# Modulation rows in four column groups of TensorE, shift and scale moved into the evictions, and recurrent columns first in the second input projection

## What is computed

```python
# block 1
mod = silu(c) @ ada_w + ada_b                       # one row of 6 x 1024
sh1, sc1, g1, sh2, sc2, g2 = split(mod, 6)
h = layer_norm(x) * (1 + sc1) + sh1
proj = h @ w_in + b_in                              # 8728 columns: attention inputs and gates
...                                                 # two attentions, merged
x = layer_norm(ALPHA * x + (1 + g1) * (merged @ w_out)) * ln1_g + ln1_b
h = layer_norm(x) * (1 + sc2) + sh2
x = layer_norm(ALPHA * x + (1 + g2) * moe(h)) * ln2_g + ln2_b   # 32 experts, 2 per token
# block 2
p = rms_norm(x) @ w_in_2                            # 256 q, 768 convolution, 1536 recurrent columns
x = x + concat(memory_attention(q), conv(pc), rwkv(pr)) @ w_out_2
x = x + expert_choice_ffn(rms_norm(x))              # 16 experts
out = rms_norm(x)
```

## Time and profile before

| | us |
|---|---|
| median of 3 runs | 2116.62 (2116.36 to 2118.09) |
| profiled execution | 2113.64 |
| its span, first to last instruction | 2111.8 |
| TensorE busy in it | 1617.2 |
| VectorE busy | 566.2 |
| ScalarE busy | 332.0 |
| granted TensorE clock, mean | 0.892 of full |

### The profile page before, as it was taken

How to read it: one execution, slowest core, us unless ns; L and a number is a source line. 1 busy time by engine, 2 the same in 40 slices (tenths; PEclk the granted TensorE clock), 3 DMA queues, 4 the chain that set the end, 5 groups by cost and what they waited for, 6 DMA issues and landing times.

```text
span 2111.8 us, 20549 instructions
## 1 busy us (share of the span) xinstructions
PE 1617.2 (77%) x8115; PEld 902.6 (43%) x8115; DVE 566.2 (27%) x1063; ACT 332.0 (16%) x699; POOL 159.7 (8%) x275
## 2 busy tenths in 40 slices
PE   7999988989978777777774976787786766666664
PEld 2746856776354222222221855566644212122111
DVE  1011243311321221211214047788742000000002
ACT  0101224510012111111111131122202000000000
POOL 3000030000000000000000002213300000000000
PEclk9999988989998999999997986888896888888887
DMA  9742342226361999999997430000002899999995
GB/s 356 182 169 82 111 171 100 71 94 218 107 255 39 428 428 429 428 429 428 429 428 288 144 120 1 1 11 1 1 33 97 353 429 429 427 429 429 428 428 245
DMA packets 84964, 510.90 MB, mean 242 GB/s; under 512 B 9543, under 2 KB 12392, under 8 KB 60326
## 3 DMA queue, kind: packets, MB, share of 16 engines
q1 hardware_dynamic: 80950, 500.21, 58.2%
q0 software_dynamic: 3952, 9.83, 2.0%
HBM read 506.87 MB, written 3.15 MB: 242 GB/s over the span
## 4 chain that ended last, share of the span: by engine, by line
PE 51%; DMA 32%; DVE 7%; issue 5%; ACT 3%; POOL 1%; SPq 1%; DVEq 0%; POOLq 0%; ACTq 0%
PE ps L1130 48%; DMA ring<-in_exp_w 16%; DMA ring<-in_w_e_up 15%; ACT arena L1054 1%; PE ps L1525 1%; POOL arena L706 1%; DMA ring<-in_ada_w 1%; DMA arena<-in_causal 0%; POOL arena L710 0%; DVE stats L1892 0%; DVE vv L2403 0%; PE ps L1160 0%; SPq L532 0%; SPq L570 0%; PE ps L1797 0%
## 5 line engine op out<-in xcount | busy, mean ns | idle before, releaser
L1130 PE MATMUL ps<-ring,arena 128*32 128x512 f32 (+4 forms) x3540 | 559.1, 673 | 203.8 <-DMA ring<-in_w_e_up 105.2
L1130 PEld LDWEIGHTS ps<-ring,arena 128*32 128x32 f32 (+2 forms) x3540 | 169.3, 132 | 549.6 <-issue 400.2
L1130 PE MATMUL ps<-arena 128*128 128x128 f32 (+7 forms) x1320 | 238.3, 354 | 52.0 <-POOL arena L706 21.5
L1130 PE MATMUL ps<-hTs,ring 128*128 128x256 f32 x1088 | 242.9, 384 | 5.9 <-PE ps L1130 3.7
L1130 PEld LDWEIGHTS ps<-hTs,ring 128*128 128x128 f32 x1088 | 208.1, 192 | 40.2 <-issue 11.8
L1130 PEld LDWEIGHTS ps<-arena 128*128 128x128 f32 (+3 forms) x1320 | 177.1, 212 | 104.9 <-issue 46.7
L1525 PE MATMUL ps<-arena 128*128 128x512 f32 x256 | 117.5, 601 | 29.0 <-DVE arena L2179 29.0
L1130 PE MATMUL ps<-ring,hTs 128*128 128x512 f32 (+4 forms) x352 | 118.4, 492 | 8.1 <-ACT hTs L1064 5.8
L2179 DVE COPY arena<-ps 128x512 f32<-128x512 f32 x32 | 22.1, 691 | 339.9 <-PE ps L1130 339.9
L2491 DVE TENSOR_TENSOR arena<-arena,ps 64x512 f32<-64x512 f32 x16 | 11.0, 690 | 357.7 <-ACT arena L1085 357.7
L1130 PEld LDWEIGHTS ps<-ring,hTs 128*128 128x128 f32 x352 | 64.3, 212 | 60.6 <-issue 52.8
(11 more groups left out here) (388 smaller groups left out, 1258.4 us busy)
## 6 DMA issues: line engine op xcount, KB each, us to landing
ring<-in_exp_w SPq DMA_DIRECT2D x96, 2048.0 KB, 20.7
ring<-in_w_e_gate SPq DMA_DIRECT2D x32, 2048.0 KB, 18.8
ring<-in_w_e_up SPq DMA_DIRECT2D x32, 2048.0 KB, 23.3
ring<-in_w_e_down SPq DMA_DIRECT2D x32, 2048.0 KB, 23.8
ring<-in_w_in SPq DMA_DIRECT2D x22, 2048.0 KB, 14.8
ring<-in_ada_w SPq DMA_DIRECT2D x12, 2048.0 KB, 8.5
ring<-in_w_out SPq DMA_DIRECT2D x4, 2048.0 KB, 7.9
ring<-in_w_br_hg SPq DMA_DIRECT2D x2, 2048.0 KB, 14.8
```

What stands on the lines that cost most here:

```text
L1130: return nc.tensor.matmul(o, lhsT, rhs, start=start, stop=stop)
```

## The change

**First part.** The modulation products use four column groups: silu(c) is spread over 32 columns, the eight products of a tile go to four groups of 32 partitions, two each, and the bias row goes to the first group. A bank then holds four partial rows. `mod_columns` turns shift and scale into columns: 16 products of a 128-column piece of the row with one column of ones on partitions 0, 32, 64 and 96, which sums the four and transposes. `mod_rows` does the sum for the gates: two products of 512 columns to all 128 partitions. The whole-matrix modulation on DVE is gone; the transposes take the normalized matrix, and scale and shift are applied per partition when the banks are emptied, two of four banks by ACT and two by DVE. In the compact form of expert stage 1 the gathered tokens get scale and shift at their eviction, too, which moves ACT's 16 evictions into the branch.

The order changes with it: the first transposes stand between the second and third tile, and all eight later tiles stand together ahead of the output projection, with `w_out` behind them in the ring.

**Second part.** In w_in_2 the three tiles with recurrent columns come first, then queries with the first convolution tile, and the last tile (two banks, `in2b`) is computed after `vt`. On DVE `prepare(0, ..)`, the reciprocal and the key's scaling stand ahead of the memory scores. On ACT the first `decays(0)` stands ahead of the memory exponentials. Two buffers move, since `hT` stays in use longer.

```diff
@@ the order of jobs and of weights @@
-PLAN1 = [("mod", 4), ("cols", 1), ("rel", 1), ("hT", 4), ...
+PLAN1 = [("mod", 2), ("hT", 4), ("modb", 2), ("modc", 1), ("cols", 1), ("rel", 1), ...
-         ("g1", 2), ("y", 4), ("mod2", 6), ("memT", 4), ("km", 1), ("vm", 2),
+         ("ada2", 8), ("g1b", 2), ("modc2", 1), ("g2b", 2), ("y", 4), ("memT", 4), ("km", 1), ("vm", 2),
-PLAN2 = [("h3T", 4), ("in2", 10), ...
-         ("kks", 2), ("vt", 2), ("matt", 10), ...
+IN2 = (2, 3, 4, 0, 1)
+PLAN2 = [("h3T", 4), ("in2", 8), ...
+         ("kks", 2), ("vt", 2), ("in2b", 2), ("matt", 10), ...
@@ TensorE @@
-                mm(bank(j), ones_row, brow_at(n)[1], True, False)
+                mm(bank(j, rows=32), ident[0:1, 0:1].to_broadcast([1, 32]), brow_at(n)[1], True, False)
                 for k in range(KC):
-                    ins = mm(bank(j), c[:, k, :], slot(n, (8, 512))[:, k, :], False, k == KC - 1)
+                    q = k % 4
+                    ins = mm(bank(j)[32 * q:32 * q + 32, :], c[:, k, :], slot(n, (8, 512))[:, k, :],
+                             0 < k < 4, k >= 4)
...
+            group = C("fold")[:, 0:1]
+            def mod_columns(name, shift, scale, every):
+                j = job(name)
+                for k in range(KC):
+                    for i, row in enumerate((shift, scale)):
+                        part = row[:, k::KC] if every else row[:, k * P:(k + 1) * P]
+                        ins = mm(bank(j)[:, 8 * i + k:8 * i + k + 1], part, group)
+                fills(ins, j)
+            def mod_rows(name, row):
+                for i in range(2):
+                    j = job(name, i)
+                    fills(mm(bank(j), group.to_broadcast([P, P]), row[:, i * 512:i * 512 + 512]), j)
...
-            for i in range(2):
-                modulation("g1", i, cbc2)
+            for i in range(8):
+                modulation("ada2", i, cbc2)
+            all_out(pe, "ada2", 8)
+            mod_rows("g1b", mod2[:, 0, :])
+            mod_columns("modc2", mod2[:, 1, :], mod2[:, 2, :], True)
+            mod_rows("g2b", mod2[:, 3, :])
             pe.wait_ge(S("merged_ready"), 1)
...
-            for i in range(6):
-                modulation("mod2", i, cbc2)
@@ ScalarE @@
+            act.wait_ge(S("modc_ready"), 1)
+            for j in (0, 2):
+                is_full(act, J("hT", j))
+                for i in range(2):
+                    k = 2 * j + i
+                    ins = nc.scalar.activation(hT[:, k, :], v3(bank(J("hT", j)), 2)[:, i, :], ACT.Identity,
+                                               bias=modc[:, k:k + 1], scale=modc[:, 8 + k:9 + k])
+                frees(ins, J("hT", j))
@@ VectorE @@
-            for t in range(TT):
-                link(stt(xn[:, t, :], mod1[:, 1, :], 1.0, xn[:, t, :], ALU.add, ALU.mult))
-            say(tt(xn[:], xn[:], mid(mod1[:, 0, :], TT), ALU.add), "h_ready")
+            layer_norm(xn, x, "xn_ready")
+            mod_column_pairs(J("modc"), modc)
+            modulated("hT", modc)
...
+            mod_column_pairs(J("modc2"), modc2)
             dve.wait_ge(S("mem_loaded"), 16)
...
+            all_out(dve, "w0", 2)
+            prepare(0, 0)
+            dve.wait_ge(S("kk_roots"), 2)
+            link(nc.vector.reciprocal(KKs, KKs))
+            link(tt(KKn, KKn, KKs, ALU.mult))
+            all_out(dve, "a0", 2)
+            for part in range(1, 4):
+                prepare(0, part)
             mem_scores(0)
             mem_scores(1)
+            all_out(dve, "in2b", 2)
```

More of the change, by code:

```diff
@@ L761, in _ @@
             nc.scalar.activation(lb, lb, ACT.Sigmoid).then_inc(S("lb_sigmoid"), 1)
-            for j in range(4):
-                is_full(act, J("hT", j))
-                frees(nc.scalar.copy(hT[:, 2 * j:2 * j + 2, :], v3(bank(J("hT", j)), 2)), J("hT", j))
             def pair(job, j, dst, func, stack_col):
@@ L880, in _ @@
             for i in range(8):
-                j = J("g1", i) if i < 2 else J("mod2", i - 2)
-                is_full(act, j)
-                frees(nc.scalar.copy(mod2[:, i // 2, (i % 2) * 512:(i % 2) * 512 + 512], bank(j)), j)
+                parts(J("ada2", i), mod2, i)
+            for i in range(2):
+                parts(J("g1b", i), mod2, i)
+            for i in range(2):
+                parts(J("g2b", i), mod2, 6 + i)
             for j in range(4):
@@ L894, in _ @@
                 frees(nc.scalar.copy(vm[:, t, :], bank(J("vm", t), 256)), J("vm", t))
-            for j in range(4):
+            act.wait_ge(S("modc_ready"), 2)
+            for j in (0, 2):
                 is_full(act, J("h2T", j))
-                frees(nc.scalar.copy(hT[:, 2 * j:2 * j + 2, :], v3(bank(J("h2T", j)), 2)), J("h2T", j))
+                for i in range(2):
+                    k = 2 * j + i
+                    ins = nc.scalar.activation(hT[:, k, :], v3(bank(J("h2T", j)), 2)[:, i, :], ACT.Identity,
+                                               bias=modc2[:, k:k + 1], scale=modc2[:, 8 + k:9 + k])
+                frees(ins, J("h2T", j))
             act.wait_ge(S("route_max"), 1)
@@ L903, in _ @@
             frees(nc.scalar.copy(combT, bank(J("combT"), T, NE1)), J("combT"))
-            for i in range(16):
-                is_full(act, J("comb", i))
-                frees(nc.scalar.copy(WB[:, 2 * i:2 * i + 2, :], v3(bank(J("comb", i)), 2)), J("comb", i))
             def silus(turn, at):
@@ L919, in _ @@
             with act.If(fits > 0):
+                for i in range(16):
+                    k = i // 2
+                    is_full(act, J("comb", i))
+                    frees(nc.scalar.activation(XE1[:, k, (i % 2) * 512:(i % 2) * 512 + 512], bank(J("comb", i)),
+                                               ACT.Identity, bias=modc2[:, k:k + 1], scale=modc2[:, 8 + k:9 + k]),
+                          J("comb", i))
                 with act.Fori(0, NE1 // 2) as i:
@@ L928, in _ @@
             with act.If(fits < 1):
+                for i in range(16):
+                    is_full(act, J("comb", i))
+                    frees(nc.scalar.copy(WB[:, 2 * i:2 * i + 2, :], v3(bank(J("comb", i)), 2)), J("comb", i))
                 silus(0, 0)
@@ L960, in _ @@
             nc.scalar.activation(PF[:, 11, :], PF[:, 11, :], ACT.Sigmoid).then_inc(S("tanh_ready"), 1)
+            is_full(act, J("in2", 6))
+            frees(nc.scalar.copy(qa, v3(bank(J("in2", 6)), 2)), J("in2", 6))
+            is_full(act, J("in2", 7))
+            frees(nc.scalar.copy(CA[:, 0:2, :], v3(bank(J("in2", 7)), 2)), J("in2", 7))
             def low_rank(name, dst, func, stack_col):
@@ L2321, in _ @@
             mem_scores(3)
-            prepare(0, 0)
             mem_probs(2)
-            dve.wait_ge(S("kk_roots"), 2)
-            link(nc.vector.reciprocal(KKs, KKs))
             for c in range(3):
```

134 lines of the change are left out of this document (77 added, 57 removed).

## The result

The changed kernel takes 2065.89 us (median of 4 runs, 2064.03 to 2070.15), against 2116.49 for the one before in the same session: a ratio of 0.9763, 95% interval 0.9745 to 0.9781. Forecast were 2063.4 and a range of 2052 to 2081. The ratios leave out two executions that stand far apart from their fellows, one of `part1` at 4980.15 us and one of the kernel before, in the same session, at 2224.27. The profiled execution has a span of 2068.3 us, 43.5 less than the 2111.8 of before.

What follows compares the result with a forecast made beforehand. TensorE's path ahead of the expert stages, which run as fast as weights arrive, was taken as the bound. Gains of 16.2 + 25.3 + 11.7 = 53.2 us off the 2116.62 median gave 2063.4 us, range 2052 to 2081.

Steps and rivals of the forecast that it cites:

- Price of a tile: One modulation tile of ada_w on TensorE: 3.25 us with column groups instead of 8.46; 6.5 at 1.2 GHz.
- Place one: Ahead of the first projection: it starts at 42.8 instead of 60.02; less 1.0 of clock, gain 16.2 us.
- Place two: Between branch products and router: h2 transposes start at 592.5, not 618.80; less 1.0 of clock, gain 25.3 us (16 to 30).
- a lone tile lands in 7.9: At place two: ada 8's weights, issued at 507.6, land 7.9 us later, before TensorE has finished ada 7.
- Columns, 5.6: Each column job turning shift and scale into columns takes 5.6 us at mixed clock; 3.9 at full, 7.2 at low.
- VectorE next in line, covered by 1.8: At place two: normalizing the residual twice takes 16.9 us, under TensorE's 18.7 by 1.8.
- Place three: Between second input projection and scan: low-rank products and scores start earlier, work leaves the memory attention; gain 11.7 us (9 to 13).
- Low clock throughout: Rival: all modulation tiles at 6.5 us; place two loses 1.6, place one gains 10.4; total 2096 us; chance 0.07.
- Weights one at a time: Rival at place two: transfers of ada 8 to 11 don't overlap, each 7.9 us behind the last; 2071 us; chance 0.10.
- Place three moves its wait: Rival: memory scores wait for DVE, its queue having the preparation first; only some 3 us remain; 2072 us; chance 0.10.
- Columns nearly free: Rival: one moving column costs only its issue, both column jobs vanish at most; 2052 us; chance 0.03.
- Signs of being wrong: Column jobs over 7.2 us, last ada tile landing after 535 (old scale), or ends_ready after the memory attention.

Runs made afterwards that it cites:

- part1: Changed kernel with the second input projection as before, so the modulation change alone; 0.983 of the kernel before.
- ahead: Changed kernel with the eight later bias rows loaded in one transfer long before, on GpSimd's queue; 2058.64 us, 0.9726 of the kernel before.
- full: Changed kernel with modulation products sent to all 128 columns again, no column groups, rest of the change kept; 2117.89 us, 1.0012 of the kernel before.
- again: Changed kernel run once more, nothing edited, for the scatter; 2068.22 us, 0.9773 of the kernel before.
- part2: Kernel before with only the second input projection's new order, modulation as before; 2102.83 us, 0.9935 of the kernel before.
- strides: Changed kernel with the column jobs' pieces swapped: neighbours at place two, every eighth element at place one; no total time given, neighbours' job 4.01 us.
- cols2: Changed kernel with each column job done twice; no total time given, second round 5.3 us at place one and 7.6 at place two.
- rows2: Changed kernel with shift and scale at place two summed as rows, VectorE modulating the matrix as before; 2066.47 us, 0.9766 of the kernel before.
- tcols: Changed kernel with each column job as 16 transposes, VectorE adding the four groups; 2067.59 us, 0.9767 of the kernel before.
- early: Changed kernel with the later bias rows issued two tiles behind their weights; 2069.35 us, 0.9784 of the kernel before.

## Why the prediction came out right, step by step

- **What bounds the kernel**: right. The stretches that hold the expert stages kept their lengths to 0.5 us, and the time saved ahead of them arrived at the end.
- **Price of a tile**: right. 3.20 us from tile to tile (`ahead`), 3.25 forecast; by `full` this is worth more than the whole gain of the first part.
- **Place one, 16.2**: the start came 16.3 earlier, where 17.2 was forecast. The 0.9 is the relative bias product, which did not fit under the evictions. The first projection tile then takes 15.75 in place of 14.07, 1.7 where 1.0 was charged: 14.6. By ada 4 only 0.6 of the 1.7 is left. In `again` the start came 13.6 earlier.
- **Place two, 25.3**: failed by size, just outside its range of 16 to 30. The h2 transposes came 31.4 us earlier, 15.7 more than the stage's start. The terms: last landing 31.5 us behind the stage's start where 27.9 was forecast, 3.6; last tile and its copy 6.4 for 4.0, 2.4; rows and columns 12.55 for 9.5, 3.0; memory block 20.1 for 18.4, 1.7; less the 1.0 charged. The memory block's 1.7 is scatter of the clock and not the change: `part2`, unedited there, has the same 8.83 for its first half, `part1` and `ahead` have 7.14. The step that failed is "a lone tile lands in 7.9": SyncE was in the way as I had it, but the memory matrix came first and the rate was 387 GB/s, not 428. I had rightly seen that the bias row holds ada 8; that the wait was a bias row's and not the transfers', and worth 11 us, only `ahead` showed.
- **Columns, 5.6**: 5.28 and 7.53. The mechanism, light work at mixed clock, holds for place one. At place two it was wrong: the stride of the loads sets it (`strides`). At either place what is paid for is the load of 128 columns (`cols2`); the price taken from the 24-column rows came near it where the clock was mixed.
- **VectorE next in line, covered by 1.8**: it ended its second norm at 584.05, 3.3 ahead of TensorE.
- **Router**: 1.5 lost there that the sum did not have, 1.15 of it in the route product, 4.88 us at a clock of 0.74 (4.78 in `part2`).
- **Place three, 11.7**: 13.3. Low-rank start 18.1 earlier in its stage, as forecast; 30 records took 5.60 and not 6.6; 7.0 came out of the memory attention, 6.8 forecast.
- **Rivals.** Low clock throughout: partly true, three of the last four tiles ran near half clock, at some 6 us (last tile, second rows, memory block) and not 33. The Trainium skill, TensorE: Matmul & The Clock Gate, HAM oscillation, by which bursts shorter than the waits between them start at low clock and which I set aside with the experts' bursts, fits here: the bursts behind waits of 2.84 and 2.53 us took 3.46 and 3.64, in `ahead`, without them, 1.92. Setting it aside was a misreading: the expert burst of 3.64 stood behind a wait of 1.21, shorter than itself, and the one behind 2.90 was the slow one. Weights one at a time: no, they landed 5.4 apart. Place three moves its wait: no, 1.45 us of waiting for TensorE remain. Columns nearly free: no (`cols2`). Slower: no.
- **Signs of being wrong**: two of the three that the prediction named came true, both at place two. The last ada tile landed at 519.9, which is 535.6 on the old scale (after 535), and a column job took 7.53 (more than 7.2). The output projection started at 538.82 where some 529 was forecast, the h2 transposes at 587.39 where some 576 was.

The sum was 10 us too high on the profiled execution (53.2 against 43.5): place two over by 11 with the router, place three under by 1.6. On the medians (50.6, and 48 by the ratio of `again`) it was 3 to 5 too high, since the profiled executions show 7 us less gain than the medians do. The total came out better than its largest term, and that is luck: place two missed by 11 us, more than the total did on any count.

## What to carry to other kernels

Before costing a fold that takes work off one engine, ask which engine is the bound. At place two the column job put 7.53 us on TensorE, the bound one, to spare VectorE 4.8 us that were covered; `rows2` loses nothing without it, and only the narrower products paid. A 2 KB load here arrived with the 2 MB issued before it on its queue: load such rows ahead. Price a matmul with few columns by its weight loads and their stride, and once the gains are down to some 5 us compare stages in the traces, since the clock of light stretches scatters the total by as much.

## What the runs showed of the hardware

- A record of a float32 matmul with one moving column, with its load of 128 columns, took 0.125 us for neighbours at a clock of 0.91 and 0.217 at 0.50 (`strides`, `again`), and 0.235 to 0.242 us for columns 32 bytes apart at clocks from 0.83 to 0.50. A transpose of 128 columns in one record took 0.12 to 0.13 for either (`tcols`).
- A 2 KB load issued behind 2 MB on its queue was there after 9.3 us (`early`).
- Modulation tiles, cut from a wider matrix in rows of 2 KB, came at 387 GB/s, the experts' tiles at 427 to 429; why was not tested.
- The same instructions at the same place were granted 0.50 or 0.68 of the clock in two executions.
